# Even layer: one projection unit ahead of the key transposes on TensorE, the sums of squares ahead of the first placed level on VectorE

## The chip, the cores and the metric

The kernel runs on one core of a Trainium2 chip. The metric is the device time of one execution in microseconds; lower is better. A core has five engines that work through their own instruction streams and wait for each other by semaphores: TensorE (PE), VectorE (DVE), ScalarE (ACT), GpSimd (POOL) and SyncE (SP), which here only issues transfers.

## What is computed

A trunk of two layers over 256 frames of width 1024. Each layer is a pre-norm, a combined input projection, two sequence mixers side by side, an output projection with a residual add, and a mixture of experts. The change touches the even layer's mixers: sliding-window attention (8 query heads, 2 key heads, head size 64) and the gated linear recurrence.

```
def even_layer_mixer(h, w_in, w_out, a_q_gain, a_k_gain, a_sinks, b_lower_bound, b_out_gain):
    a_q, a_k, a_v, b_q, b_f, b_i, b_g = _split(h @ w_in, EVEN_SPLITS)
    o_a = sliding_window_sink_attention(a_q, a_k, a_v, a_q_gain, a_k_gain, a_sinks)
    o_b = hgrn2_recurrence(b_q, b_f, b_i, b_g, b_lower_bound, b_out_gain)
    return jnp.concatenate([o_a, o_b], axis=-1).astype(h.dtype) @ w_out

# in sliding_window_sink_attention:
    q = rms_norm(q.reshape(b, s, A_Q_HEADS, A_HEAD_DIM), q_gain).astype(F32)
    k = rms_norm(k.reshape(b, s, A_KV_HEADS, A_HEAD_DIM), k_gain).astype(F32)
    scores = jnp.einsum('bncgrd,bnkgd->bngrck', qb, kw) * (A_HEAD_DIM ** -0.5)
    ...
    probs = jax.nn.softmax(jnp.concatenate([scores, sink], axis=-1), axis=-1)[..., :-1]
    out = jnp.einsum('bngrck,bnkgd->bncgrd', probs, vw)
```

The recurrence is, per head, S_t = diag(f_t) S_{t-1} + (1-f_t) i_t^T and o_t = S_t^T q_t, in chunks of 64 frames.

## The kernel before

The input projection of the even layer is cut into 8 chunks of up to 384 columns, and each chunk into 4 units: `units(c, j)` on PE multiplies the rows 2j and 2j+1 (in blocks of 128) of chunk c. A weight is used as a high part WH (written by ACT, `split_hi`, L592) and a low part WL (written by DVE, `split_lo`, L606), and each product is three matmuls (L610 to L612). `split(c, j)` on ACT and on DVE makes unit (c, j) ready, six units are buffered, and ACT evacuates a chunk's banks when its last unit is done (`evacuate`).

The order of work on each engine is written out by hand. Into the stream of projection units PE mixes the work of the two mixers, whose inputs are ready by then:

- Recurrence: seven levels. For level L, POOL takes differences of the running log decay (`DL`, L777 and L778, semaphore `b_d`), ACT takes their exponential (`b_exp`), DVE multiplies them by queries and keys (`b_factors(L)`, semaphore `b_ml`, from level 4 on POOL waits for it), PE multiplies (`b_level(L)`, L2210, semaphore `b_mm`), and DVE places the block into the matrix `AT` by a predicated copy (`b_place(L)`, L1654, semaphore `b_cp`). `b_level(L)` waits for `b_cp` to reach L-1, so `b_level(3)` waits for `b_place(1)`.
- Attention: ACT squares queries and keys (`SQA`), DVE sums the squares (`qk_sums()`, L1306, semaphore `sumsq`), POOL scales and takes the power -0.5 for 20 columns (`rsqrt`, L690 and L691, ahead of its level 6), DVE multiplies the keys (`normed_keys()`, four products into `KD`, semaphore `a_qk`), PE transposes them (`k_T()`, four transposes, L1947), ACT copies them to `KTT` (`k_rows()`, L1081), PE makes the scores (`scores(0)`, `scores(1)`, from L2260 on), DVE takes the maxima (`softmax_max`), ACT the exponentials (`softmax_exp`), DVE divides (`softmax_norm`), and PE transposes the probabilities (`probs_T`, L1947).

The semaphore waits of the key transposes and of the scores:

```
def k_T():
    pe.wait_ge(sem("a_qk"), 4)
    pe.wait_ge(sem("a_QT"), 1)
def scores(i):
    pe.wait_ge(sem("a_QT"), 3)
    if i:
        pe.wait_ge(sem("proj_ev"), outs_before[0, "in", 7])
```

PE's stream around the change runs `units(5, 1)`, `b_level(3)`, `units(5, 2)`, `k_T()`, `units(5, 3)`, `scores(0)`, `units(6, 0)`, `b_level(4)`, `units(6, 1, 2)`, `b_level(5)`, `units(6, 3)`, `probs_T(0)`, `units(7, 0)`, `scores(1)`. DVE's stream runs `split(5, 2)`, `b_place(1)`, `qk_sums()`, `split(5, 3)`, `split(6, 0)`, `b_place(2)`, `b_factors(4)`, `normed_keys()`, `split(6, 1)`, `b_factors(5)`, `split(6, 2, 3)`, `softmax_max(0)`. ACT's stream has `k_rows()` behind `split(6, 2, 3)`, and behind it `b_exp(5)`, `evacuate(0, 5)` and `split(7, 0, 1)`. SP issues the transfer of the first output chunk when `split(5, 3)` is done; the experts' transfers are issued when the slots they go to have been used.

Of the kernel before, what the change touches and what calls it, by code (L numbers as in the profile page):

```python
# [117 lines left out]
def program(nc, x, mix_norm, moe_norm, ev_w_in, ev_w_out, a_q_gain, a_k_gain, a_sinks, b_lb_logits,  # L118
# [4 lines left out]
    with ctx:  # L123
# [43 lines left out]
        def mask(level):  # L167
            return MK[:, level, :]
# [102 lines left out]
        def sem(name):  # L271
            if name not in sems:
                sems[name] = ctx.enter_context(nc.semaphore(name))
            return sems[name]

        def done(ins, name, n=1):

            ins.then_inc(sem(name), n)
            cnt[name] = cnt.get(name, 0) + n
            return cnt[name]  # L280
# [39 lines left out]
        for layer in (0, 1):  # L320
            for what, chunks in (("in", CHUNKS[layer]), ("out", OUT_CHUNKS)):
                for c, (kind, _, w) in enumerate(chunks):
                    outs_before[layer, what, c] = o
                    o += NT if kind == "tok" else w // P
# [14 lines left out]
        def bank_free(layer, what, c, n_out):  # L339


            mine = {bank_of(layer, what, c, n) for n in range(n_out)}
            last = 0
            for e in range(c):
                kind, _, w = (CHUNKS[layer] if what == "in" else OUT_CHUNKS)[e]
                for n in range(NT if kind == "tok" else w // P):
                    if bank_of(layer, what, e, n) in mine:
                        last = outs_before[layer, what, e] + n + 1
            return last
# [248 lines left out]
        def split_lo(dve, i, j):  # L598
            u = unit_no[i, j]
            dve.wait_ge(sem("unit_hi"), u + 1)  # L600
            raw, hi, lo = unit_views(i, j)
            if scaled(i, j):
                done(nc.vector.scalar_tensor_tensor(out=lo, in0=raw, scalar=BCOLG, in1=hi.bitcast(F32), op0=ALU.mult,
                                                    op1=ALU.subtract), "unit_lo")
            else:
                done(nc.vector.tensor_tensor(out=lo, in0=raw, in1=hi.bitcast(F32), op=ALU.subtract), "unit_lo")  # L606
# [18 lines left out]
        def project_unit(pe, layer, what, c, j):  # L625

                kind, _, w = (CHUNKS[layer] if what == "in" else OUT_CHUNKS)[c]
                i = slot_of[layer, what, c]
                n_out = NT if kind == "tok" else w // P
                u = unit_no[i, j]  # L630
                order = sorted(range(4), key=lambda jj: unit_no[i, jj])
                first, final = 2 * order[0], 2 * order[3] + 1
                pe.wait_ge(sem("unit_lo"), u + 1)
                wh = WH[:, u % UNITS, 0:2 * w].rearrange("p (k n) -> p k n", k=2)
                wl = WL[:, u % UNITS, 0:2 * w].rearrange("p (k n) -> p k n", k=2)
                for kk in range(2):
                    k = 2 * j + kk
                    for n in range(n_out):
                        bank = bank_of(layer, what, c, n)
                        if kind == "tok":  # L640
                            ts = slice(n * P, (n + 1) * P)
                            last = product(PS[:, bank, 0:w], HTH[:, k, ts], HTL[:, k, ts], wh[:, kk, :], wl[:, kk, :],
                                           k == first, k == final)
                        else:
                            cs = slice(n * P, (n + 1) * P)
                            nc.tensor.matmul(PS[:, bank, 0:T], wh[:, kk, cs], HTH[:, k, :], start=k == first, stop=False)  # L646
                            nc.tensor.matmul(PS[:, bank, 0:T], wh[:, kk, cs], HTL[:, k, :], start=False, stop=False)  # L647
                            last = nc.tensor.matmul(PS[:, bank, 0:T], wl[:, kk, cs], HTH[:, k, :], start=False,  # L648
                                                    stop=k == final)
                done(last, "unit_used")  # L650
# [640 lines left out]
        def _(dve):  # L1291
# [13 lines left out]
            def total(out, a, op=ALU.add):  # L1305
                return nc.vector.tensor_reduce(out=out, in_=a, axis=AX, op=op)  # L1306
# [244 lines left out]
            def split(c, *js):  # L1551
                for j in js:
                    split_lo(dve, slot_of[0, "in", c], j)
# [45 lines left out]
            def qk_sums():  # L1599
                dve.wait_ge(sem("a_sq"), 1)  # L1600
                done(total(ASS, SQA[:, :, :].rearrange("p i (h n) -> p (i h) n", n=64)), "sumsq")
# [33 lines left out]
            def b_factors(L):  # L1635

                dve.wait_ge(sem("b_e"), L - 1)
                if L >= 3:
                    dve.wait_ge(sem("b_mm"), L - 1)
                c = 2 ** L  # L1640
                ev, mv, qv, kv = (a.rearrange("p (n c) -> p n c", c=c) for a in (
                    DL[:, L % 2, :], ML[:, L % 2, :], TQ[:, :, :].rearrange("p h t -> p (h t)"),
                    KH[:, :, :].rearrange("p h t -> p (h t)")))
                tt(mv[:, :, c // 2:], ev[:, :, c // 2:], qv[:, :, c // 2:], MUL)
                done(tt(mv[:, :, 0:c // 2], ev[:, :, 0:c // 2], kv[:, :, 0:c // 2], MUL), "b_ml")

            def b_place(L):

                dve.wait_ge(sem("b_mm"), L + 1)
                dve.wait_ge(sem("b_cp"), L)  # L1650
                c = 2 ** L
                sh = [P, 8, P // c, c // 2]
                m1 = mask(L - 1).rearrange("p (m c) -> p m c", c=c)[:, :, c // 2:]
                done(nc.vector.copy_predicated(at8.rearrange("p n (m c) -> p n m c", c=c)[:, :, :, c // 2:],  # L1654
                                               m1.unsqueeze(1).to_broadcast(sh),
                                               PS[:, 6 + L % 2, :].rearrange("p (n m c) -> p n m c", n=8, c=c // 2)), "b_cp")
# [22 lines left out]
            split(5, 0, 1)  # L1679
            b_factors(3)  # L1680
            split(5, 2)
            b_place(1)
            qk_sums()
            split(5, 3)
            split(6, 0)
            b_place(2)
# [255 lines left out]
        def _(pe):  # L1942
# [243 lines left out]
            def units(c, *js):  # L2186
                for j in js:
                    if j == 0:
                        pe.wait_ge(sem("proj_ev"), bank_free(0, "in", c, NT))
                    project_unit(pe, 0, "in", c, j)  # L2190
# [9 lines left out]
            def b_level(L):  # L2200

                pe.wait_ge(sem("b_ml"), L)
                if L >= 2:
                    pe.wait_ge(sem("b_cp"), L - 1)
                m, c = ML[:, L % 2, :], 2 ** L
                for i in range(NT):
                    for h in range(4):
                        fr = m[:, h * T + i * P:h * T + (i + 1) * P]
                        n = 4 * i + h
                        last = mm(PS[:, 6 + L % 2, CH * n:CH * (n + 1)].rearrange("p (m c) -> p m c", c=c // 2),  # L2210
                                  KH[:, h, i * P:(i + 1) * P] if L == 1 else fr,
                                  fr.rearrange("p (m c) -> p m c", c=c)[:, :, c // 2:], start=True, stop=True)
                done(last, "b_mm")
# [26 lines left out]
# [3 lines that stand above are left out]
                transposes(4, [(PS[:, 4, g * T + i * P:g * T + i * P + P], KD[:, i, g, :, :].rearrange("p d n -> p (d n)"))  # L2243
                               for g in range(2) for i in range(NT)], "a_T")
# [65 lines left out]
            q_T(1)  # L2310
            units(5, 1)
            b_level(3)
            units(5, 2)
            k_T()
            units(5, 3)
            scores(0)
            units(6, 0)
            b_level(4)
            units(6, 1, 2)
            b_level(5)  # L2320
# [278 lines left out]
```

## Time and profile before

| | us |
|---|---|
| Median of 3 runs | 586.52 (586.25 to 588.19) |
| The profiled execution | 586.91 |
| Its span | 584.7 |
| PE busy | 541.3 (93%) |
| DVE busy | 328.9 (56%) |
| ACT busy | 254.0 (43%) |
| POOL busy | 81.4 (14%) |

The mean granted clock of PE over the span is 0.975. A busy share is an average over stages with different limits; what decides is who waits for whom in the stage that is changed. The even layer's input projection with the mixers runs from about 10 to 107 us of the span.

### The profile page before, as it was taken

How to read it: one execution, taken by the hardware profiler on the slowest of the kernel's cores; microseconds unless marked ns; L12 is line 12 of the kernel's file. 1: busy time of each engine (PE TensorE's matmuls, PEld its weight loads, DVE VectorE, ACT ScalarE, POOL GpSimd, SP SyncE). 2: the span in 40 equal slices, each digit the busy share in tenths (PEclk: the TensorE clock that was granted, in tenths of full speed). 3: DMA queues.
4: the chain of work that ended last, by engine and by line, in shares of the span. 5: the costliest groups of instructions: out<-in, count | busy, mean ns of one | idle time of the engine just before them, and what ended most of it. 6: DMA issues, size and time to landing. Idle time of an engine off the chain costs nothing.

```text
span 584.7 us, 12159 instructions
## 1 busy us (share of the span) xinstructions
PE 541.3 (93%) x5162; PEld 445.5 (76%) x5162; DVE 328.9 (56%) x595; ACT 254.0 (43%) x501; POOL 81.4 (14%) x98
## 2 busy tenths in 40 slices
PE   6999799999899999789999999999999889999975
PEld 6999799996565645359989998999889656664632
DVE  3579876657334333377996555467445633334335
ACT  5576467664233323155546434433226323331311
POOL 5716621100000000021003900011110000000000
PEclk9999999998999999999999799999789989999999
DMA  9991333787899999997463430000315979989992
GB/s 319 272 371 58 108 109 110 228 305 295 312 408 409 375 411 409 390 376 243 160 215 80 176 109 2 4 4 2 145 34 225 411 282 411 408 347 412 407 409 109
DMA packets 55671, 144.16 MB, mean 247 GB/s; under 512 B 4292, under 2 KB 29088, under 8 KB 55488
## 3 DMA queue, kind: packets, MB, share of 16 engines
q1 hardware_dynamic: 54496, 141.88, 64.6%
q0 software_dynamic: 944, 1.41, 1.2%
q8 instruction: 42, 0.69, 0.5%
q10 hardware_dynamic: 176, 0.07, 0.1%
q14 instruction: 13, 0.11, 0.1%
HBM read 142.30 MB, written 1.05 MB: 245 GB/s over the span
## 4 chain that ended last, share of the span: by engine, by line
PE 75%; DVE 14%; ACT 5%; issue 3%; POOL 1%; DMA 1%; ACTq 0%; DVEq 0%
PE PS L2097 11%; PE PS L2058 7%; PE PS L2119 6%; PE PS L610 6%; PE PS L611 5%; PE PS L612 5%; PE PS L2133 4%; PE PS L646 3%; DVE WL L606 3%; PE PS L648 2%; PE PS L647 2%; PE PS L2134 2%; PE PS L2467 2%; PE PS L2488 2%; DVE SL L1303 2%
## 5 line engine op out<-in xcount | busy, mean ns | idle before, releaser
L606 DVE TENSOR_TENSOR WL<-RAW,WH 128x768 fp32r<-128x768 f32 (+2 forms) x90 | 82.0, 947 | 30.2 <-ACT WH L592 29.8
L610 PE MATMUL PS<-WH,HTH 128*128 128x384 f32 (+2 forms) x272 | 93.2, 343 | 3.0 <-DVE HTL L1295 1.4
L611 PE MATMUL PS<-WL,HTH 128*128 128x384 f32 (+2 forms) x272 | 90.1, 331 | 0.0
L612 PE MATMUL PS<-WH,HTL 128*128 128x384 f32 (+2 forms) x272 | 90.0, 331 | 0.0
L1295 DVE TENSOR_TENSOR X<-PS,X 128x512 f32<-128x512 f32 (+2 forms) x84 | 53.9, 663 | 48.0 <-PE PS L2134 36.1
L592 ACT ACTIVATE WH<-RAW 128x768 fp32r<-128x768 f32 (+2 forms) x90 | 67.2, 793 | 4.8 <-PE PS L612 3.1
L610 PEld LDWEIGHTS PS<-WH,HTH 128*128 128x128 f32 x272 | 53.5, 197 | 4.4 <-DVE HTL L1295 1.7
L611 PEld LDWEIGHTS PS<-WL,HTH 128*128 128x128 f32 x272 | 53.7, 197 | 0.0
L992 ACT ACTIVATE SIL<-PS,MW 128x128 f32<-128x128 f32 x18 | 6.6, 367 | 107.6 <-PE PS L2097 98.0
L612 PEld LDWEIGHTS PS<-WH,HTL 128*128 128x128 f32 x272 | 53.3, 196 | 0.0
L646 PE MATMUL PS<-HTH,WH 128*128 128x256 f32 x160 | 46.0, 287 | 0.4 <-DVE HTL L1303 0.4
L648 PE MATMUL PS<-HTH,WL 128*128 128x256 f32 x160 | 45.3, 283 | 0.0
L647 PE MATMUL PS<-HTL,WH 128*128 128x256 f32 x160 | 45.3, 283 | 0.0
L1303 DVE SCALAR_TENSOR_TENSOR HID<-SIL,MW,PS 128x128 f32<-128x128 f32 x18 | 6.3, 348 | 64.3 <-ACT SIL L992 64.3
L2133 PE MATMUL PS<-YH,PTR 128*128 128x512 f32 x64 | 29.9, 467 | 10.2 <-issue 5.6
L1295 DVE TENSOR_TENSOR YL<-PS,YH 128x512 fp32r<-128x512 f32 x36 | 24.9, 692 | 20.9 <-ACT YH L1004 19.0
L2133 PEld LDWEIGHTS PS<-YH,PTR 128*128 128x128 f32 x64 | 12.0, 187 | 30.2 <-issue 25.1
L2097 PE MATMUL PS<-XG,GT 128*32 128x256 f32 x512 | 30.7, 394 | 2.0 <-issue 2.0
L1004 ACT ACTIVATE YH<-PS 128x512 fp32r<-128x512 f32 x36 | 21.5, 597 | 24.7 <-PE PS L2119 24.7
L646 PEld LDWEIGHTS PS<-HTH,WH 128*128 128x128 f32 x160 | 30.7, 192 | 0.8 <-DVE HTL L1303 0.8
L647 PEld LDWEIGHTS PS<-HTL,WH 128*128 128x128 f32 x160 | 30.7, 192 | 0.0
L648 PEld LDWEIGHTS PS<-HTH,WL 128*128 128x128 f32 x160 | 30.7, 192 | 0.0
(362 smaller groups left out, 1060.8 us busy)
## 6 DMA issues: line engine op xcount, KB each, us to landing
RAW<-moe_w_down SPq DMA_DIRECT2D x32, 512.0 KB, 13.1
RAW<-moe_w_gate SPq DMA_DIRECT2D x32, 512.0 KB, 7.8
RAW<-moe_w_up SPq DMA_DIRECT2D x32, 512.0 KB, 8.6
XD<-moe_w_down SPq DMA_DIRECT2D x32, 512.0 KB, 13.4
XG<-moe_w_gate SPq DMA_DIRECT2D x32, 512.0 KB, 9.2
XG<-moe_w_up SPq DMA_DIRECT2D x32, 512.0 KB, 10.3
RAW<-od_w_in SPq DMA_DIRECT2D x9, 1536.0 KB, 7.8
RAW<-ev_w_in SPq DMA_DIRECT2D x5, 1536.0 KB, 15.4
```

What stands on the lines that cost most here:

```text
L592: done(nc.scalar.activation(hi, raw, ACT.Copy, scale=BCOLG if scaled(i, j) else 1.0), "unit_hi")
L606: done(nc.vector.tensor_tensor(out=lo, in0=raw, in1=hi.bitcast(F32), op=ALU.subtract), "unit_lo")
L610: nc.tensor.matmul(ps, ah, bh, start=start, stop=False)
L611: nc.tensor.matmul(ps, ah, bl, start=False, stop=False)
L612: return nc.tensor.matmul(ps, al, bh, start=False, stop=stop)
L646: nc.tensor.matmul(PS[:, bank, 0:T], wh[:, kk, cs], HTH[:, k, :], start=k == first, stop=False)
L647: nc.tensor.matmul(PS[:, bank, 0:T], wh[:, kk, cs], HTL[:, k, :], start=False, stop=False)
L648: last = nc.tensor.matmul(PS[:, bank, 0:T], wl[:, kk, cs], HTH[:, k, :], start=False, stop=k == final)
L1295: return nc.vector.tensor_tensor(out=out, in0=a, in1=b, op=op)
L2058: last = mm(bank[:, kk * T:kk * T + w], part[:, i, k * P:(k + 1) * P], pf[:, i, :], start=n == 0, stop=n == 3)
L2097: last = mm(PS[s, 0, T * (t % 2):T * (t % 2) + T], GT[:, g % 2, k, o + s.start:o + s.stop], w, start=k == 0, stop=k == KT - 1)
L2133: mm(bank, at_, YH[:, 512 * b:512 * b + 512], start=True, stop=False)
```

## The change

Two lists of calls are reordered; no instruction is added or taken away. On PE `units(5, 3)` goes ahead of `k_T()`, and `units(6, 0)` goes between `k_T()` and `scores(0)`. On DVE `qk_sums()` goes ahead of `b_place(1)`.

```diff
@@ vector engine
             b_factors(3)
             split(5, 2)
+            qk_sums()
             b_place(1)
-            qk_sums()
             split(5, 3)
             split(6, 0)
             b_place(2)
@@ tensor engine
             q_T(1)
             units(5, 1)
             b_level(3)
-            units(5, 2)
+            units(5, 2, 3)
             k_T()
-            units(5, 3)
+            units(6, 0)
             scores(0)
-            units(6, 0)
             b_level(4)
             units(6, 1, 2)
             b_level(5)
```

## Rows read from the trace of the kernel before

**Rows 1.** The page: granted clock in 40 slices, and the chain's shares by engine.
```profile
PEclk9999999998999999999999799999789989999999
...
PE 75%; DVE 14%; ACT 5%; issue 3%; POOL 1%; DMA 1%; ACTq 0%; DVEq 0%
```

**Rows 2.** The chain that ended last, 58 to 72 us: start, us, what.
```profile
60.88 1.24 DVE AT L1654
62.12 1.25 DVE SM L1306
...
64.39 4.15 POOL SM L691
...
68.56 2.62 DVE KD L1295 x4
```

**Rows 3.** PE in order of time: start, us, line, tiles, count, idle before and its releaser.
```profile
63.58 1.89 PE L2210 MATMUL PS<-ML 128*128 128x64 f32 x16
65.28 0.42 PE L610 MATMUL PS<-WH,HTH 128*128 128x384 f32 x1
...
67.28 0.34 PE L612 MATMUL PS<-WH,HTL 128*128 128x384 f32 x1
71.22 1.11 PE L1947 MATMUL PS<-CT,KD 128*128 128x128 f32 x4 [3.61 <-DVE KD L1295]
71.99 0.67 PE L610 MATMUL PS<-WH,HTH 128*128 128x384 f32 x1
...
75.41 0.27 PE L2262 MATMUL PS<-KTT,QT 64*64 64x64 f32 x1
...
88.55 1.03 PE L1947 MATMUL PS<-CT,SB 128*128 128x128 f32 x8
...
90.94 0.27 PE L2262 MATMUL PS<-KTT,QT 64*64 64x64 f32 x1
```

**Rows 4.** Stage table: stretch, us, busy of PE, PEld, DVE, ACT, POOL, clock, DMA.
```profile
67.60:71.20 3.60, 0.01 (x1) 0.00 (x0) 2.64 (x5) 0.00 (x0) 3.02 (x3) 0.98 0.84 311
71.20:74.40 3.20, 3.17 (x12) 3.18 (x13) 1.54 (x4) 1.63 (x2) 0.00 (x0) 0.50 0.02 5
```

**Rows 5.** POOL in order of time, around the change and in the odd layer.
```profile
61.81 1.04 POOL L778 TENSOR_TENSOR DL<-LB 128x512 f32<-128x512 f32 x1
63.46 0.85 POOL L690 TENSOR_SCALAR SM<-SM 128x20 f32<-128x20 f32 x1 [0.61 <-DVE SM L1306]
...
68.51 1.06 POOL L777 TENSOR_TENSOR DL<-LB 128x512 f32<-128x512 f32 x1
...
382.55 0.21 POOL L690 TENSOR_SCALAR SM<-SM 128x8 f32<-128x8 f32 x1 [47.47 <-DVE SM L1306]
382.84 1.65 POOL L691 TENSOR_TENSOR SM<-SM 128x8 f32<-128x8 f32 x1
```

**Rows 6.** DVE in order of time, 63 to 93 us.
```profile
63.28 1.81 DVE L606 TENSOR_TENSOR WL<-RAW,WH 128x768 fp32r<-128x768 f32 x2
...
66.76 0.68 DVE L1295 TENSOR_TENSOR ML<-DL,KH 128x512 f32<-128x512 f32 x1
...
74.04 0.69 DVE L1295 TENSOR_TENSOR ML<-DL,TQ 128x512 f32<-128x512 f32 x1 [1.59 <-ACT DL L1068]
...
77.41 1.21 DVE L1306 TENSOR_REDUCE SM<-PS 128x8 f32<-128x1024 f32 x1
...
83.66 1.23 DVE L1295 TENSOR_TENSOR SB<-SB,SM 128x1024 f32<-128x1024 f32 x1
...
92.22 1.23 DVE L1306 TENSOR_REDUCE SM<-PS 128x8 f32<-128x1024 f32 x1 [4.93 <-PE PS L2264]
```

**Rows 7.** ACT in order of time, the copy of the transposed keys.
```profile
72.38 0.69 ACT L1081 ACTIVATE KTT<-PS,PT 128x512 f32<-128x512 f32 x1 [7.58 <-PE PS L1947]
```

**Rows 8.** PE in order of time, in the odd layer's output projection.
```profile
432.34 0.44 PE L610 MATMUL PS<-WH,HTH 128*128 128x384 f32 x1 [1.41 <-DVE HTL L1295]
```

**Rows 9.** Stage table, the stretch behind that row.
```profile
432.89:436.30 3.41, 3.41 (x13) 3.41 (x12) 3.02 (x6) 0.13 (x1) 1.00 (x1) 0.50 0.00 0
```

## Prediction

> **What bounds the kernel now.** I read the page first. The chain that ended last is TensorE (PE) for 75% of the span, and the granted clock is full in most slices [rows 1]. So only time on PE's own line counts: where PE stands idle, and where it runs at the lower clock. The list of waits then shows one long idle of PE in the even layer, 3.61 us ahead of the four transposes of `k_T()`, ended by VectorE (DVE) writing KD, the normed keys [rows 3]. I took the chain of that stretch next [rows 2]. It comes back to PE only at 71.22 [rows 3]. Before that run `b_place(1)` (60.88 to 62.12), the sums of squares `qk_sums()` (to 63.37), the scaling (from 63.46 [rows 5]) and the power -0.5 (to 68.54) on GpSimd (POOL), and the four products of `normed_keys()` (68.56 to 71.18). Third, the stage table shows what the idle costs beyond itself: the clock is granted at 0.98 in the idle stretch and at 0.50, the lower of its two levels (1.2 of 2.4 GHz), from 71.20 to 74.40, with PE busy for all of it [rows 4]. Last, DVE, POOL and ScalarE (ACT) in order of time show who is free when [rows 5 to 7].
>
> **PE's order: `units(5, 3)` ahead of `k_T()`.** No instruction is added or removed, the order changes. A unit of this width takes from 65.28 to 67.28 plus a last step of 0.17, so 2.17 us at full clock [rows 3]. In the kernel before, `units(5, 3)` runs behind the stall, from 71.99 to 75.41, 3.42 us, because most of it falls into the low clock [rows 3, 4]. Moved ahead, it runs from 67.45 to 69.62, where PE now stands still. Its split half WL must be there: it is the first of the two splits that run on DVE from 63.28 to 65.09 [rows 6], long before. So 3.42 us go from behind the stall. The four transposes took 0.77 us at the low clock (71.22 to 71.99), at the full clock half of that, 0.38: 0.39 us go.
>
> The copy of the transposed keys to KTT on ACT now starts at 72.38 [rows 7], 1.16 us after the transposes start; `scores(0)` needs it. Its cover was `units(5, 3)`; now it is `units(6, 0)`, another 2.17 us of PE. With transposes at 70.2 the copy runs from about 70.9 to 71.6, and PE comes to `scores(0)` at 70.17 + 0.38 + 2.17 = 72.7. It costs nothing; without that cover it would cost about 1.1 us. `units(6, 0)` needs its own split, the second of those at 63.28, and the banks of chunk 4, which ACT empties ahead of the squares that the sums read: both are there. Queued on ACT behind the waiting copy stand the exponential of level 5, the evacuation of chunk 5 and the splits of chunk 7; all of them come earlier, none later.
>
> **DVE's order: `qk_sums()` ahead of `b_place(1)`.** The sums end 1.24 us earlier, at about 62.2 [rows 2]. POOL can't use all of it: its level 5 differences end at 61.81 + 1.04 = 62.85 [rows 5]. So the scaling starts at 62.85, not 63.46. It took 0.85 us for 20 columns, and 0.21 us for 8 columns at 382.55 [rows 5]; the difference lies beside the split that starts at 63.28. If it starts at 62.85 it is over before that split. Then the power begins at 63.14 and, at its 4.15 us [rows 2] (8 columns took 1.65 [rows 5], the same per column), ends at 67.29. DVE is then still busy with `b_factors(4)` until 66.76 + 0.68 = 67.44 [rows 6], so the products of `normed_keys()` start at about 67.45 to 67.5, 1.05 us earlier. If the scaling keeps its 0.85 us, it is 62.85 + 0.85 + 0.08 + 4.15 = 67.94, only 0.6 earlier. If the sums free nothing, it is 0. I take 1.05, as the short scaling is the row without a neighbour. The products themselves keep their 2.62 us, since POOL's level 6 differences, which two of them wait for (start 68.51, 1.06 us each [rows 5]), wait for `b_factors(4)` too and also come 1.05 earlier.
>
> The Trainium skill ("SBUF — State Buffer", section "Who interferes with whom") says that a DVE instruction with two SBUF inputs excludes a GpSimd instruction that reads SBUF, that `tensor_reduce` never does, and that whoever starts first keeps the port for its whole instruction. The first half agrees with the scaling's 0.85 against 0.21 us. The last part would speak against this change, and it is a rival below.
>
> What the swap moves back: `b_place(1)` ends 1.25 us later, at about 63.4. `b_level(3)` on PE waits for it and starts at 63.58 [rows 3]. That is 0.2 us of room. If it is late, PE only comes later to `k_T()`, where 0.55 us of idle are left, so the first 0.5 us cost nothing. `split(5, 3)` and all behind it on DVE start when they did, and SP's transfer of the first output chunk, which waits for that split, too.
>
> **The sum.** 3.42 + 0.39 + 1.05 = 4.86 us. Seen from the other side: `k_T()` starts at 70.17; PE reaches it at 69.62; the idle falls from 3.77 to 0.55 us (3.22) and the low clock goes (1.25 on the unit, 0.39 on the transposes). Same sum. With 0.6 for DVE it is 4.4, with 0 it is 3.8.
>
> **Who is late next.** The chain on ACT and DVE moves less than PE: by 1.05 plus about 0.45 for the faster transposes, 1.5 us. Level 5 products 74.04 to 72.5, the maximum of the first scores 77.41 to 75.9 (its scores start at 72.7), the product that ends `softmax_norm(0)` from 83.66 + 1.23 = 84.89 to 83.4 [rows 6]. PE reaches `probs_T(0)` at 88.55 - 4.86 = 83.7 [rows 3]: 0.3 us of room, the tightest place. `scores(1)` goes from 90.94 to 86.1; DVE stood idle 4.93 us for it [rows 6] and still has 1.6 us left. So the whole 4.86 us reach the second softmax, and from there everything hangs on it in one piece: the recurrence, the output projection, the router. SP issues the expert loads as PE and DVE use up the slots, so they move along.
>
> The profiled execution took 586.91 us for a span of 584.7. 586.91 - 4.86 = 582.05. It stood 0.4 above the median of the runs; I put the forecast between the two, at 581.9.
>
> **The rivals.**
> - *The swap on DVE pays nothing* (POOL or DVE is late for another reason). Against it: POOL's idle of 0.61 us ahead of the scaling ended with the sums [rows 5]. Time 583.1. Chance 0.06.
> - *The clock falls all the same.* PE still stands idle 0.55 us, and the key transposes are short work. For it: after 1.41 us of idle ahead of 432.34 [rows 8] the clock stood at 0.50 from 432.89 to 436.30 [rows 9]. Against it: 0.55 is well under that, in an otherwise dense stretch. It would fall on the transposes and `units(6, 0)` and cost the 1.64 us back: 583.7. Chance 0.07. The Trainium skill ("TensorE: Matmul & The Clock Gate", section "Why this matters for your kernels") warns only of gaps about the size of the one removed; rows 8 and 9 show the low level after a shorter one, so the rows decide and the case keeps its chance.
> - *The softmax chain becomes the bound* at `probs_T(0)`. Beyond the 0.3 us of room each us late costs one; a slip of 1.2 gives 583.0. Chance 0.04.
> - *Slower: the power on POOL keeps DVE out.* It now starts at 63.14, ahead of `split(5, 3)` at 63.28. If it held the shared port for all of its 4.15 us, that split would start at 67.29, and the 4.16 us of DVE work from 63.28 to 67.44 would end at 71.45. The keys would be ready at 74.1 and PE would stand idle from 70.4. `k_T()` is 2.9 us later than now, 3.42 go, and `units(6, 0)` runs at the low clock (+1.25): 0.8 us slower, 587.7. It decides at whether the power starts before 63.28. Against it: in the trace of before the power ran from 64.39 to 68.54, and a product of `b_factors(4)` with both inputs in SBUF took its usual 0.68 us inside it [rows 2, 6]. Chance 0.03. By the page's rule on whole instructions this would be the outcome; those rows speak against it.
> - *Given back later*: PE meets other gaps at other moments, and the low clock stretches of the page [rows 1] (each 3.4 us costs 1.7) fall differently. Three more give it all back, 586.5: chance 0.05. More than that is slower by over 0.3%: 0.02.
>
> **How the numbers follow.** Forecast 0.73. A measurement of this kernel tells about 0.3%, 1.8 us, from no change. The forecast and the first three rivals are faster by more than that: 0.90. The slower rival (+0.8) and the gain given back are within it: 0.08; slower 0.02. The range 580.4 to 584.3 holds the forecast with one low stretch fewer or more, the DVE bounds, and the three rivals at 583 to 583.7.
>
> **What would show it.** In the trace after: `units(5, 3)` back to back behind `units(5, 2)`; the idle ahead of the key transposes 0.4 to 1.1 us; no matmul of 0.52 us behind them; the scaling on POOL near 0.2 us at 62.9 and the power ending by 67.3; `b_level(3)` at 63.6; no idle ahead of `probs_T(0)`; `scores(1)` at 86.1. The prediction is wrong if a new idle of PE over 0.5 us stands anywhere between 72 and 100 us, or if splits on DVE behind 63.3 us take far over 0.9 us each.

## Result and the profile after

The changed kernel takes 580.37 us in the median of its runs, against 585.63 us for the kernel before on the same chips. The ratio is 0.9914, with a 95% interval of 0.9891 to 0.9937: 5.0 us faster, between 3.7 and 6.4. Ratios here and below leave out the few slow runs, which are over 1.5% above the fastest of their kernel. Its profiled execution took 580.04 us, for a span of 577.9.

The stretch of the change is best measured by itself, from the start of the second transposes of the queries (`q_T(1)`, ahead of everything that is moved) to the start of the transposes of the first probabilities (`probs_T(0)`, behind it). In the kernel before it begins with this row, and ends at 88.55 [rows 3]:

```profile
61.06 0.60 PE L1947 MATMUL PS<-CT,TA 128*128 128x128 f32 x4
```

That is 27.49 us. PE in order of time in the kernel after (start, us, engine, line, tiles, count; an idle before a row would stand in brackets):

```profile
61.60 0.60 PE L1947 MATMUL PS<-CT,TA 128*128 128x128 f32 x4
...
64.20 1.97 PE L2210 MATMUL PS<-ML 128*128 128x64 f32 x16
65.98 0.42 PE L610 MATMUL PS<-WH,HTH 128*128 128x384 f32 x1
...
70.23 0.60 PE L1947 MATMUL PS<-CT,KD 128*128 128x128 f32 x4
70.58 0.42 PE L610 MATMUL PS<-WH,HTH 128*128 128x384 f32 x1
...
72.87 0.27 PE L2262 MATMUL PS<-KTT,QT 64*64 64x64 f32 x1
...
74.01 2.00 PE L2210 MATMUL PS<-ML 128*128 128x64 f32 x16
...
83.94 1.03 PE L1947 MATMUL PS<-CT,SB 128*128 128x128 f32 x8
...
86.33 0.27 PE L2262 MATMUL PS<-KTT,QT 64*64 64x64 f32 x1
```

From 61.60 to 83.94 is 22.34 us: 5.15 us less. No row has a bracket. Two units run from 65.98, `k_T()` follows at 70.23 without a wait, `units(6, 0)` covers the copy to KTT. The stage table over the same stretches as [rows 4] (us, busy of PE, PEld, DVE, ACT, POOL, then the granted clock, DMA share, GB/s):

```profile
67.60:71.20 3.60, 3.60 (x24) 3.57 (x23) 3.53 (x8) 0.34 (x1) 2.76 (x2) 1.00 0.96 357
71.20:74.40 3.20, 3.20 (x62) 2.88 (x61) 2.36 (x4) 3.20 (x7) 0.51 (x1) 1.00 0.03 8
```

PE is busy throughout and at the upper level of its clock. DVE and POOL around the moved sums:

```profile
61.34 1.47 DVE L1306 TENSOR_REDUCE SM<-SQA 128x20 f32<-128x1280 f32 x1
62.74 1.32 DVE L1654 COPY_PREDICATED AT<-MK,PS 128x512 f32<-128x512 uint8 x1
63.85 1.85 DVE L606 TENSOR_TENSOR WL<-RAW,WH 128x768 fp32r<-128x768 f32 x2
...
67.38 0.67 DVE L1295 TENSOR_TENSOR ML<-DL,KH 128x512 f32<-128x512 f32 x1
67.97 0.88 DVE L1295 TENSOR_TENSOR KD<-TA,SM 128x128 f32<-128x128 f32 x4
```
```profile
63.48 0.21 POOL L690 TENSOR_SCALAR SM<-SM 128x20 f32<-128x20 f32 x1
63.78 3.57 POOL L691 TENSOR_TENSOR SM<-SM 128x20 f32<-128x20 f32 x1
68.12 1.76 POOL L777 TENSOR_TENSOR DL<-LB 128x512 f32<-128x512 f32 x1 [0.78 <-DVE ML L1295]
```

Two things are to be seen. The scaling takes 0.21 us, as forecast. And the four products into KD take 0.88 us where they took 2.62 [rows 2]; this was not forecast. Now it is POOL's first level 6 instruction that is long, 1.76 against 1.06 us [rows 5].

The span fell by 6.8 us, more than the stretch. The clock row of the profile's page shows where the rest may lie:

```profile
PEclk9999999997999999999999799999999899999999
```

Behind the stretch it has three slices under 9, against five in [rows 1]; two of the three stand at the same places. I don't put that part down to the change: another trace of the same kernel (both_again) has four such slices, and the kernel's own runs vary with the clock, from 578.8 us at a mean granted clock of 0.984 to 587.1 at 0.967. The stretch repeats better: 22.34 us in both traces of the changed kernel. But every other kernel has one trace only. Below both are given, the stretch and the whole time.

### The profile page after: what moved, and what is told of

It is laid out like the page before. It is cut to its first block, busy times and chain, and to the rows that moved or that the text cites. A ratio compares the mean times of both kernels' runs of the same rounds, so it can differ in the third digit from the quotient of the medians.

```text
span 577.9 us, 12159 instructions
## 1 busy us (share of the span) xinstructions
PE 537.5 (93%) x5162; PEld 443.3 (77%) x5162; DVE 329.2 (57%) x595; ACT 254.2 (44%) x501; POOL 81.3 (14%) x98
## 3 DMA queue, kind: packets, MB, share of 16 engines
HBM read 142.30 MB, written 1.05 MB: 248 GB/s over the span
## 4 chain that ended last, share of the span: by engine, by line
PE 82%; DVE 9%; ACT 4%; issue 3%; DMA 1%; ACTq 0%; DVEq 0%
PE PS L2097 11%; PE PS L2058 8%; PE PS L610 7%; PE PS L612 7%; PE PS L611 7%; PE PS L2119 6%; PE PS L2133 4%; PE PS L646 3%; PE PS L648 3%; PE PS L647 3%; PE PS L2134 2%; PE PS L2466 2%; PE PS L2487 2%; DVE SL L1303 2%; PE PS L2475 2%
## 5 line engine op out<-in xcount | busy, mean ns | idle before, releaser
L610 PE MATMUL PS<-WH,HTH 128*128 128x384 f32 (+2 forms) x272 | 90.9, 334 | 3.0 <-DVE WL L606 1.6
L612 PE MATMUL PS<-WH,HTL 128*128 128x384 f32 (+2 forms) x272 | 88.5, 325 | 0.0
L611 PE MATMUL PS<-WL,HTH 128*128 128x384 f32 (+2 forms) x272 | 88.5, 325 | 0.0
L610 PEld LDWEIGHTS PS<-WH,HTH 128*128 128x128 f32 x272 | 52.2, 192 | 4.3 <-DVE HTL L1295 1.7
L611 PEld LDWEIGHTS PS<-WL,HTH 128*128 128x128 f32 x272 | 52.1, 191 | 0.0
L612 PEld LDWEIGHTS PS<-WH,HTL 128*128 128x128 f32 x272 | 52.0, 191 | 0.0
L2097 PE MATMUL PS<-XG,GT 128*32 128x256 f32 x512 | 29.3, 380 | 2.2 <-issue 2.2
```

What stands on the lines that cost most here:

```text
L610: nc.tensor.matmul(ps, ah, bh, start=start, stop=False)
L611: nc.tensor.matmul(ps, ah, bl, start=False, stop=False)
L612: return nc.tensor.matmul(ps, al, bh, start=False, stop=stop)
L2097: last = mm(PS[s, 0, T * (t % 2):T * (t % 2) + T], GT[:, g % 2, k, o + s.start:o + s.stop], w, start=k == 0, stop=k == KT - 1)
```

## The experiments

Saved in the stretch, against 27.49 us, and what PE shows ahead of the key transposes. What each kernel is stands with its experiment below:

| kernel | start to end of the stretch | us | saved | idle ahead of `k_T()` | products into KD |
|---|---|---|---|---|---|
| after | 61.60 to 83.94 | 22.34 | 5.15 | none | 0.88 |
| both_again | 61.10 to 83.44 | 22.34 | 5.15 | none | 0.90 |
| pe_alone | 61.19 to 85.11 | 23.92 | 3.57 | 1.54 | 2.6 |
| dve_alone | 60.45 to 83.58 | 23.13 | 4.36 | 0.55 | 0.90 |
| filled | 60.85 to 86.88 | 26.03 | 1.46 | 0.52, 3.29 filled | 2.61 |
| pool_after_keys | 60.53 to 86.35 | 25.82 | 1.67 | 1.90 | 0.90 |
| pe_pool | 61.99 to 84.19 | 22.20 | 5.29 | none | 0.90 |
| both_pool | 61.64 to 83.97 | 22.33 | 5.16 | none | 0.88 |
| both_pause | 60.62 to 83.78 | 23.16 | 4.33 | 0.58 | 1.69 |
| dve_pause | 61.60 to 86.85 | 25.25 | 2.24 | 2.67 | 1.69 |
| no_cover | 60.93 to 84.53 | 23.60 | 3.89 | 0.24 | 2.62 |
| no_cover_pool | 61.11 to 84.31 | 23.20 | 4.29 | none | 0.88 |
| two_ahead | 61.70 to 86.80 | 25.10 | 2.39 | none | 2.62 |

The whole times follow this table only loosely. For six of these kernels the 95% interval of the whole saving does not hold what the stretch saves: pool_after_keys (2.0 to 4.3 us by the whole time) gained more, and pe_pool (0.7 to 4.0), both_pool (0.1 to 3.8), both_pause (at most 4.3), dve_pause (at most 1.6) and no_cover_pool (0.6 to 3.9) gained less. Where the rest went behind the stretch was not looked for. So the table shows what each order is worth in the stretch, and not how much of it the whole kernel keeps. The full size in the whole time is shown for the changed kernel only: 5.0 us from 21 runs, and again in both_again.

### The parts, and whether they add

Each part of the diff alone:

> The order of PE's stream as in the changed kernel, DVE's as before. Theory: the keys are ready at the old moment, 3.75 us after units(5, 2) ends, so PE still stands idle about 1.55 us behind units(5, 3), the products into KD keep 2.6 us, and the clock stays full: 3.42 + 0.39 = 3.8 us faster than before. Rival (the clock falls after this idle all the same): the transposes and units(6, 0) run at half clock, 2.2 us faster than before.

> The order of DVE's stream as in the changed kernel, PE's as before. Theory from the trace after: DVE comes to the products into KD straight from b_factors(4), ahead of POOL's level 6 differences, so they take 0.9 us, not 2.6; the keys are ready at about 68.35 on the old scale, PE is idle 0.9 us instead of 3.6, the clock stays full: 2.9 + 1.64 = 4.5 us faster than before, nearly all of the change. Rival (the prediction's step, products at 2.62 us): key transposes at 70.2, idle 2.7 us, 1.05 us faster, or 2.7 if the clock stays full.

> The changed kernel itself, beside its two parts. Theory: 5.0 to 5.3 us faster than before, no idle ahead of the key transposes; the two parts overlap, so it is only 0.5 to 1 us ahead of the DVE part alone and 1.5 ahead of the PE part alone. Rival (the parts add): PE part 3.8 and DVE part 1.05.

Medians: 580.11 for the PE part (ratio 0.9897, interval 0.983 to 0.9965), 580.01 for the DVE part (0.9938, 0.9896 to 0.998), 579.70 for both (0.9896, 0.9839 to 0.9954), against 584.70 before. The whole times don't part them; the stretch does: 3.57, 4.36 and 5.15 us. The parts don't add. Both fight the same idle, and one of them is nearly enough. PE and DVE with the DVE part alone:

```profile
67.75 0.66 PE L1947 MATMUL PS<-CT,KD 128*128 128x128 f32 x4 [0.55 <-DVE KD L1295]
```
```profile
66.20 0.68 DVE L1295 TENSOR_TENSOR ML<-DL,KH 128x512 f32<-128x512 f32 x1
66.80 0.90 DVE L1295 TENSOR_TENSOR KD<-TA,SM 128x128 f32<-128x128 f32 x4
```

By the prediction's price for DVE (1.05 us earlier) the idle here would be 2.7 us. It is 0.55. The rival of the expectation, that the products keep their 2.62 us, falls: they take 0.90. With the PE part alone the products stay long and 1.54 us of idle are left, as expected; the clock stayed full after it:

```profile
71.36 0.66 PE L1947 MATMUL PS<-CT,KD 128*128 128x128 f32 x4 [1.54 <-DVE KD L1295]
```

### The low clock as a term of its own

The kernel before with work put into the idle (filled):

```diff
             units(5, 2)
+            pe.wait_ge(sem("a_QT"), 1)
+            for _ in range(14):
+                mm(PS[:, 4, 0:P], ident, ident, start=True, stop=True)
             k_T()
```

> The kernel before, with 14 matmuls of 128 x 128 that nobody reads put ahead of the key transposes, into the bank that these write next; they fill some 3 us of the idle. Theory: the keys come no earlier, but the clock stays full, so the transposes and units(5, 3) win 1.6 us back: 1.6 us faster than before. Rival (the low clock costs nothing there, something else waits): no difference, with units(5, 3) at 2.2 us and a new idle ahead of scores(0).

PE of this kernel; each of the 14 matmuls leaves two records:

```profile
67.25 3.29 PE L2316 MATMUL PS<-CT 128*128 128x128 f32 x28
71.06 0.66 PE L1947 MATMUL PS<-CT,KD 128*128 128x128 f32 x4 [0.52 <-DVE KD L1295]
```

The median was 583.93 against 584.70 (ratio 0.9974, 0.994 to 1.0008), not clear of no change. In the stretch 1.46 us are saved, where 1.64 were worked out, though the keys came no sooner. From the key transposes to `scores(0)` at 73.73 it is 2.67 us, against 4.19 before (71.22 to 75.41). So of the 5.15 us about 1.5 were the clock and the rest was the idle itself. The rival, a new idle ahead of `scores(0)`, did not come.

### What made the products into KD short

POOL's level 6 differences wait for the keys, first in the kernel before (pool_after_keys), then in the PE part alone (pe_pool):

```diff
                 if L >= 4:
                     pool.wait_ge(sem("b_ml"), L - 2)
+                if L == 6:
+                    pool.wait_ge(sem("a_qk"), 4)
```

> The kernel before, with one wait more: POOL begins its level 6 differences only when DVE has written the keys KD. Nothing else is changed. Theory (the 2.6 us of the products are time spent waiting for POOL's two level 6 instructions): the products take 0.9 us, the keys are ready 1.7 us earlier, PE's idle falls from 3.6 to about 1.9 us; if the clock stays full after that, another 1.6: 3.3 us faster than before, 1.7 if it falls. Rival (the products are slow by themselves, or because their input has just been written): KD still takes 2.6 us and nothing is gained.

> PE's order as in the changed kernel, DVE's as before, and the same wait on POOL. Theory: the keys are ready at about 69.5 on the old scale, PE comes at 69.6, no idle: 5.2 us faster than before from the second transposes of the queries to the transposes of the first probabilities, the same as the changed kernel without its swap on DVE. Rival (the earlier sums themselves are needed): as the PE part alone, 3.6 us.

DVE and POOL of the first (its line numbers are two higher):

```profile
68.05 0.90 DVE L1297 TENSOR_TENSOR KD<-TA,SM 128x128 f32<-128x128 f32 x4 [1.12 <-POOL SM L691]
```
```profile
69.09 1.08 POOL L779 TENSOR_TENSOR DL<-LB 128x512 f32<-128x512 f32 x1 [1.07 <-DVE KD L1297]
```

The stretch behind, by the stage table:

```profile
69.90:73.30 3.40, 3.40 (x17) 2.96 (x18) 3.03 (x4) 1.51 (x3) 2.19 (x3) 0.50 0.03 7
```

The sums, the scaling and the power are as late as before, and the products take 0.90 us. So the other 1.7 us were time spent behind POOL's two instructions, not work. The trace of the kernel before says so too, in the view of the tile KD (minimum, median and maximum in ns); its four products take from 277 to 1156 ns for the same work. The prediction had the waiting in it but not that it could go:

```profile
L1295 DVE TENSOR_TENSOR KD<-TA,SM x4: 277/699/1156, 68.6 to 70.9; 128x128 f32<-128x128 f32 x4
```

The median was 581.60 against 584.69 (0.9946, 0.9927 to 0.9966). Of the two figures given for the clock the lower one came true: it fell 0.9 us behind the 1.90 us of idle, and only 1.67 us are saved in the stretch. With PE's order changed as well (pe_pool) the stretch saves 5.29 us, as much as the changed kernel, with DVE's order left alone. The 0.14 us more are `b_level(3)`, which is on time there and takes 1.89 us instead of 1.97. Its whole time doesn't show that: 581.86 in the median against 584.69 (0.996, 0.9932 to 0.9988), with runs from 577.75 to 585.82, and the long ones at a granted clock of 0.970 to 0.972. Why so many of its runs had a lower clock was not settled.

The reverse is two instructions of 4 columns on DVE ahead of the products, in the changed kernel (both_pause) and in the DVE part alone (dve_pause):

```diff
             b_factors(4)
+            link(ts(LBM, LBC, 1.0, MUL))
+            link(ts(LBM, LBC, 1.0, MUL))
             normed_keys()
```

> The changed kernel with two instructions of 4 columns on DVE (some 0.4 us together, their result is not used) between b_factors(4) and the products into KD. Theory (POOL's level 6 differences, released by b_factors(4), and the products race for the shared port, and now POOL comes first): the products take 2.6 us again, PE stands idle 0.6 to 1.0 us ahead of the key transposes, 4.2 to 4.6 us faster than before, near the prediction's sum. Rival (the 0.9 us come from the earlier scaling or from anything else): products at 0.9 us, idle at most 0.1 us.

> The same two instructions in the kernel with the DVE part alone. Theory: products at 2.6 us, keys 0.7 us earlier than before at most, PE idle about 2.9 us instead of 0.55, and the clock falls after it or not; 0.7 us faster than before (2.3 if the clock stays full), against 4.4 without the pause. Rival: as the DVE part alone less 0.4 us, 4.0.

DVE and POOL of both_pause:

```profile
66.99 1.26 DVE L1299 TENSOR_SCALAR SM<-SM 128x4 f32<-128x4 f32 x2
68.28 1.69 DVE L1295 TENSOR_TENSOR KD<-TA,SM 128x128 f32<-128x128 f32 x4
```
```profile
67.14 1.08 POOL L777 TENSOR_TENSOR DL<-LB 128x512 f32<-128x512 f32 x1 [0.77 <-DVE ML L1295]
68.18 1.04 POOL L778 TENSOR_TENSOR DL<-LB 128x512 f32<-128x512 f32 x1
```

The pause wasn't the 0.4 us meant: its two small instructions took 1.26, since the second stood behind POOL's first level 6 instruction, and the products then stood behind only the second one (1.69, not 2.6). Taken together, from the end of `b_factors(4)` to the end of the keys, it is 2.9 us against 0.8. The idle was the 0.58 us expected, and the stretch saves 4.33. In the DVE part alone the same pause leaves 2.67 us of idle and saves 2.24, as expected for a clock that stays full. It did (stage table of dve_pause):

```profile
71.00:74.40 3.40, 3.38 (x50) 3.13 (x52) 2.19 (x5) 2.23 (x4) 0.00 (x0) 1.00 0.03 8
```

Medians: 581.15 (0.9966, 0.9927 to 1.0004) and 583.93 (1.0006, 0.9973 to 1.0039), against 584.24 before. So the PE part makes the stretch hard to upset: keys that come 2.1 us later cost 0.8 us with it, and all 2.1 without. In the changed kernel they are ready 1.4 us before `k_T()` starts (68.85 and 70.23).

Last, both_pool:

> The changed kernel, with POOL's level 6 differences waiting for the keys as well. Theory: products at 0.9 us whatever the order of start, no idle, 5.15 us faster than before from the second transposes of the queries to the transposes of the first probabilities; no difference from the changed kernel. Rival (the later differences cost something later): a new idle of DVE or ACT ahead of level 6, and slower than the changed kernel.

Here the wait is added to the changed kernel. The stretch saves 5.16 us, no difference, and PE has no idle in it; the median is 581.94 against 584.24 (0.9967, 0.9935 to 0.9998), again with runs at a low granted clock, down to 0.970. The changed kernel itself was not run beside it, so whether the wait costs something behind the stretch stays open. None of the versions tried is clearly ahead of the changed kernel.

### The cover of the copy to KTT

The changed kernel with `scores(0)` ahead of `units(6, 0)`, first as it is (no_cover), then with POOL's wait (no_cover_pool):

```diff
             k_T()
-            units(6, 0)
             scores(0)
+            units(6, 0)
```

> The changed kernel with scores(0) right behind the key transposes and units(6, 0) behind it. Theory: PE waits there for the copy to KTT, about 1.0 us, and nothing later gives it back: 4.1 us faster than before in that stretch instead of 5.15. Rival (the scores come earlier, so the softmax chain gives it back): the same as the changed kernel.

> The same, with scores(0) right behind the key transposes. Theory: no idle ahead of the transposes, about 0.8 us ahead of scores(0), given back nowhere: 4.2 us faster than before in that stretch. Rival: no difference from the changed kernel there.

The first run brought something that wasn't asked for. DVE's and POOL's orders are those of the changed kernel, and the products took 2.62 us:

```profile
67.28 2.62 DVE L1295 TENSOR_TENSOR KD<-TA,SM 128x128 f32<-128x128 f32 x4
```
```profile
67.43 1.27 POOL L777 TENSOR_TENSOR DL<-LB 128x512 f32<-128x512 f32 x1 [0.77 <-DVE ML L1295]
```

POOL's instruction starts 0.15 us behind the first product here, and 0.15 us behind it in the changed kernel (67.97 and 68.12), where all four products went through. Here two went through, and the third (67.68) and the fourth took 1.17 and 1.12 us. The programs differ only behind `k_T()` on PE, later than this. So the outcome isn't fixed by the program: both starts hang on the end of `b_factors(4)`, and it fell one way in three traces (after, both_again, dve_alone) and the other way in this one. The idle at `k_T()` was 0.24 us then, and 0.78 stood ahead of `scores(0)`. So the changed kernel may lose some 0.24 us in some of its executions; neither of its two traces shows it. POOL's wait takes this race away (no_cover_pool):

```profile
71.16 0.27 PE L2264 MATMUL PS<-KTT,QT 64*64 64x64 f32 x1 [0.78 <-ACT KTT L1083]
```

The stretch saves 4.29 us, 0.87 less than both_pool: that is what the place of `units(6, 0)` is worth, and nothing later gave it back. The medians are 580.19 against 584.69 (0.9936, 0.9906 to 0.9967) and 581.34 against 584.24 (0.9962, 0.9933 to 0.999).

### Who would be late next

The kernel before with another order on PE (two_ahead):

```diff
-            units(5, 2)
-            k_T()
-            units(5, 3)
-            scores(0)
-            units(6, 0)
-            b_level(4)
+            units(5, 2, 3)
+            units(6, 0)
+            k_T()
+            b_level(4)
+            scores(0)
```

> DVE's order as before; on PE both units(5, 3) and units(6, 0) ahead of the key transposes, and b_level(4) ahead of scores(0). Theory: no idle at the key transposes, but they and the chain of the first softmax come as late as in the kernel before, so PE, which is 5 us ahead, stands idle 1 to 1.5 us ahead of the transposes of the first probabilities: 3.7 to 4.2 us faster than before. Rival (that chain has room): 5.2 us.

```profile
72.26 0.60 PE L1947 MATMUL PS<-CT,KD 128*128 128x128 f32 x4
...
81.29 1.97 PE L2210 MATMUL PS<-ML 128*128 128x64 f32 x16 [1.19 <-DVE AT L1654]
```
```profile
83.20:86.60 3.40, 3.40 (x12) 3.40 (x12) 2.79 (x6) 2.91 (x6) 0.00 (x0) 0.50 0.28 101
```

The size of the new idle was right, its place wrong: PE waited 1.19 us ahead of `b_level(5)`, for `b_place(3)`, which stands on DVE behind the first maximum. The transposes of the probabilities came later and found their input there. And the clock fell 1.9 us after that idle had ended, which costs another 1.7 us, so only 2.39 us are saved in the stretch. The median was 580.58 against 584.69 (0.9937, 0.9903 to 0.9971). Here running ahead on PE paid only as far as DVE's chain was brought forward with it.

## Why the prediction was right, and where it was not

The forecast was 581.9 us in a range of 580.4 to 584.3. The median of 580.37 lies at its lower end, but it comes with a kernel before of 585.63 us; the forecast started from 586.52, and by the ratio that gives 581.5. The saving was 5.0 us with an interval of 3.7 to 6.4, where 4.86 had been summed, and 5.15 in the stretch. The mechanism is the forecast one, with one term wrong. That the sum came so near is in part luck: one term was 0.55 us too small, and several small ones that it left out took 0.3 back.

- *PE's order, 3.42 us and the cover.* Right. `units(5, 3)` runs in the idle, `units(6, 0)` hides the copy. The full clock on the transposes (0.39) is right too: 70.23 to 70.58 is 0.35. With pe_alone, 3.57 us came where 3.81 were forecast by these two terms. Of the 0.24 that are missing, 0.11 is `b_level(4)` (below) and 0.10 the step from the end of a unit to the scores (75.31 to 75.41 before, 73.94 to 74.04 in pe_alone), which the 3.42 us had counted in and which stays.
- *The DVE part, first step.* Right. The sums came ahead, the scaling took 0.21 us, and the power ended (67.35) before `b_factors(4)` did (68.05). It took 3.57 us, not 4.15. In the kernel before it starts at 64.39, inside a split that ends at 65.09 [rows 2, 6], so that it was probably held up as well. I had not seen this, as I took it to scale with its columns: that 8 and 20 columns gave the same time per column was chance.
- *"The products themselves keep their 2.62 us".* This step failed. DVE now comes to them without a break, ahead of POOL's level 6 differences, and they take 0.88 us. The keys are ready 1.7 us sooner than that term said, but PE can use only the 0.55 us of idle the sum had left it. That is why the error hardly shows in the time; the idle of 0.4 to 1.1 us that was to show the forecast did not appear. In dve_alone the error shows in full: 4.36 us, not 1.05 or 2.7.
- *"What the swap moves back".* Nearly right. `b_level(3)` starts 2.60 us behind the second query transposes instead of 2.52 (64.20 against 61.60; 63.58 against 61.06). It is 0.08 us late, and with no idle left these count.
- *The sum.* 4.86, plus 0.55 for the idle that went too, less the 0.08, gives 5.33; measured 5.15. The 0.18 that are missing are two rows of PE: `b_level(3)`, 1.97 us instead of 1.89, and `b_level(4)`, 2.00 us right behind the scores where it took 1.89 behind a unit.
- *Who is late next.* Right. `probs_T(0)` did not wait: the product that ends `softmax_norm(0)` is done at 83.39 and PE comes at 83.94, so there was 0.55 us of room, where 0.3 was worked out. `b_place(3)`, the one that was late in two_ahead, ends at 79.14 here, 0.93 us before `b_level(5)` at 80.07. DVE of the changed kernel:

```profile
78.43 0.71 DVE L1654 COPY_PREDICATED AT<-MK,PS 128x512 f32<-128x512 uint8 x1
...
82.16 1.23 DVE L1295 TENSOR_TENSOR SB<-SB,SM 128x1024 f32<-128x1024 f32 x1
```

- *The rival of the clock* did not come: there was no idle left to cause it. Where one was left, the clock stayed full after 0.55 us, the very length that the rival named (dve_alone), and after 0.58 (both_pause), 1.54 (pe_alone) and 2.67 us (dve_pause). After 1.90 us (pool_after_keys) it fell, and in two_ahead it fell 1.9 us behind one of 1.19 us. The length of an idle alone does not tell it.
- *The rival of POOL keeping DVE out.* The power did start before the split, 63.78 against 63.85, and both splits took 1.85 us, as before (1.81 [rows 6]). The Trainium skill ("SBUF — State Buffer", section "Who interferes with whom") says that whoever starts first keeps the port for its whole instruction. For POOL's 512 columns the rows agree: about 1.1 us for each product that stood behind them. For the power on 20 columns they don't, and here the measurement decides.

## What to carry to other kernels

An idle that ends a chain over three engines can be attacked from both ends: put independent work of the waiting engine into it, and bring the chain forward. Price the two together, since they compete for one idle, and look how each stands a delay of the chain: here keys that came 2.1 us later cost 0.8 us with both parts, and all 2.1 us with the DVE part alone. Before taking an instruction's duration as work, compare it with its fellows in the same group: four equal products in 2.62 us whose shortest took 0.28 were waiting, and a duration that is a wait moves when anything around it moves.

## What the runs showed of the hardware

A product of 128 columns on DVE takes 0.27 to 0.30 us by itself and about 1.1 us behind a POOL instruction of 512 columns (2.62 us for four, against 0.88). The other way round, POOL's instruction goes from 1.06 to 1.76 us behind DVE's. With the starts 0.15 us apart and the same order on both engines, either came out (changed kernel and no_cover). A stretch at the lower clock followed idles of 3.61 us (before), 1.90 us (pool_after_keys) and, 1.9 us later, 1.19 us (two_ahead); none followed idles of 0.55, 0.58, 1.54 and 2.67 us. Each of these is one execution.
